# Attention on one Trainium2 core: the plain query is left unnormed, its inverse norm becomes the scale of the exponential, and the rotated query part takes the quotient of both norms

## The reference, cut to what matters

```python
def mla_qk_norm(x, gain):
    return jnp.concatenate([rms_norm(x[..., :MLA_NOPE], gain[:MLA_NOPE]),
                            rms_norm(x[..., MLA_NOPE:], gain[MLA_NOPE:])], axis=-1)
...
    q = (rms_norm(cq, q_norm) @ w_uq).reshape(b, t, MLA_HEADS, MLA_NOPE + MLA_ROPE)
    q = mla_qk_norm(q, q_gain)
...
def attend(q, k, v):
    s = jnp.einsum('bqhd,bkhd->bhqk', q, k, preferred_element_type=jnp.float32) * (q.shape[-1] ** -0.5)
    p = jax.nn.softmax(s, axis=-1).astype(v.dtype)
    return jnp.einsum('bhqk,bkhd->bqhd', p, v)
```

## Time and profile before

| | |
|---|---|
| median of 3 runs | 3030.11 us (3029.92 to 3032.5) |
| profiled execution | 3029.51 us, its span 3027.9 us |
| PE busy | 2984.7 us (99%) |
| DVE busy | 1806.4 us (60%) |
| ACT busy | 859.6 us (28%) |
| POOL busy | 37.3 us (1%) |
| chain that ended last | PE 93%, DVE 4%, ACT 1%, issue 1%, DMA 1% |

### The profile page before, as it was taken

How to read it: one execution, slowest core, us unless ns; L and a number is a source line. 1 busy time by engine, 2 the same in 40 slices (tenths; PEclk the granted TensorE clock), 3 DMA queues, 4 the chain that set the end, 5 groups by cost and what they waited for, 6 DMA issues and landing times.

```text
span 3027.9 us, 42295 instructions
## 1 busy us (share of the span) xinstructions
PE 2984.7 (99%) x17472; PEld 2604.4 (86%) x17472; DVE 1806.4 (60%) x2615; ACT 859.6 (28%) x1150; POOL 37.3 (1%) x74
## 2 busy tenths in 40 slices
PE   7999999999999999999999999999999999999999
PEld 5888888888998888888888888888889888888887
DVE  5765555766676775656574556566664646554454
ACT  5111111354445421111142111113332332332221
POOL 0000000000000000000000000000000000000000
PEclk9999999999999999999999999999999999999999
DMA  6332323111101332323211223231121211122222
GB/s 268 144 129 103 111 98 110 56 53 56 56 28 57 125 138 100 123 92 116 97 70 70 97 85 123 95 113 69 56 84 42 72 53 70 70 73 94 97 97 83
DMA packets 41064, 278.08 MB, mean 92 GB/s; under 512 B 4368, under 2 KB 5648, under 8 KB 8080
## 3 DMA queue, kind: packets, MB, share of 16 engines
q1 hardware_dynamic: 31024, 205.85, 18.7%
q0 software_dynamic: 9952, 70.98, 6.5%
HBM read 274.72 MB, written 2.10 MB: 91 GB/s over the span
## 4 chain that ended last, share of the span: by engine, by line
PE 93%; DVE 4%; ACT 1%; issue 1%; DMA 1%; SPq 0%; DVEq 0%; ACTq 0%
PE ps L330 30%; PE ps L332 29%; PE ps L331 29%; PE ps L652 1%; PE ps L356 1%; DVE act_buf L1497 1%; DVE xnl L1501 1%; DMA ada_w<-ada 1%; PE ps L344 1%; DVE wl L1413 0%; PE ps L638 0%; PE ps L639 0%; ACT wh L977 0%; ACT xnh L1008 0%; DVE ssum L1476 0%
## 5 line engine op out<-in xcount | busy, mean ns | idle before, releaser
L330 PE MATMUL ps<-xnh,wl 128*128 128x512 f32 (+1 forms) x3040 | 1057.7, 348 | 11.1 <-DVE wl L1413 5.4
L331 PE MATMUL ps<-xnl,wh 128*128 128x512 f32 (+1 forms) x3040 | 1048.4, 345 | 0.0
L332 PE MATMUL ps<-xnh,wh 128*128 128x512 f32 (+1 forms) x3040 | 1047.4, 345 | 0.0
L330 PEld LDWEIGHTS ps<-xnh,wl 128*128 128x128 f32 x3040 | 577.3, 190 | 92.2 <-issue 10.3
L332 PEld LDWEIGHTS ps<-xnh,wh 128*128 128x128 f32 x3040 | 577.1, 190 | 70.1
L331 PEld LDWEIGHTS ps<-xnl,wh 128*128 128x128 f32 x3040 | 577.5, 190 | 67.7 <-issue 1.0
L977 ACT ACTIVATE wh<-raw 128x2048 fp32r<-128x2048 f32 (+2 forms) x176 | 322.7, 1833 | 552.8 <-PE ps L332 552.8
L1413 DVE TENSOR_TENSOR wl<-raw,wh 128x2048 fp32r<-128x2048 f32 (+1 forms) x178 | 393.6, 2211 | 140.7 <-ACT wh L977 140.5
L1572 DVE SCALAR_TENSOR_TENSOR h<-ps,coef,h 128x512 f32<-128x512 f32 x624 | 371.4, 642 | 105.5 <-PE ps L332 104.0
L330 PE MATMUL ps<-hidh,wl 128*128 128x512 f32 (+1 forms) x1232 | 422.2, 343 | 3.3 <-DVE h L1512 3.3
L332 PE MATMUL ps<-hidh,wh 128*128 128x512 f32 (+1 forms) x1232 | 423.3, 344 | 0.0
(11 more groups left out here) (255 smaller groups left out, 2962.4 us busy)
## 6 DMA issues: line engine op xcount, KB each, us to landing
raw<-weights SPq DMA_DIRECT2D x183, 1024.0 KB, 4.8
adaw<-ada POOLq DMA_DIRECT2D x64, 1024.0 KB, 5.1
ada_w<-ada SPq DMA_DIRECT2D x8, 1024.0 KB, 19.1
h<-x_in SPq DMA_DIRECT2D x1, 2048.0 KB, 8.7
c_act<-c_rows POOLq DMA_DIRECT2D x2, 1024.0 KB, 5.8
out<-h SPq DMA_DIRECT2D x8, 256.0 KB, 2.0
h<-x_in SPq DMA_DIRECT2D x1, 1024.0 KB, 28.6
cs<-rope_mla POOLq DMA_DIRECT2D x1, 512.0 KB, 3.7
```

Source lines behind the costliest of these rows:

```text
L330: mm(dst, lhs[1][rows], rhs[0][rows], start=first, stop=False)
L331: mm(dst, lhs[0][rows], rhs[1][rows], start=False, stop=False)
L332: return mm(dst, lhs[0][rows], rhs[0][rows], start=False, stop=last)
```

## The change

Both plain queries of a pair are no longer normed. Let r be the inverse norm of a query row. Since exp(r · s − r · max s) is the exponential of the normed scores, r goes into the exponential as its scale, and the maximum is multiplied by r. The rotated part, which is added to the same scores, then has to be divided by r: it is multiplied by its own inverse norm and the plain part's norm.

- The items change places: 0 and 1 are now the plain queries, 2 the rotated part, 3 and 4 the keys. ACT writes the high part of a plain query with its gain straight out of PSUM (`take`), DVE the rest straight out of PSUM (`query_lo`).
- PE sums the squares of both plain queries into one bank (`head_sums`), ACT takes the root of all (`q_std`), and PE turns it by four matmuls so that the norms of 128 queries stand one per partition (`turned_std`). DVE takes their reciprocals (`q_inv`, 24 columns) and multiplies the rotated part's inverse norm by `q_std`.
- Two of the five spreads go, with two `scaled`, two `hi`, two `lo` from SBUF and two reciprocals of 192 columns.
- Each of the ten tiles gets a multiplication of the maximum (two for tiles of context queries), with a wait of DVE for itself ahead of it (`step`), and the exponential gets a scale from SBUF.
- On PE the rope's spread moves behind `value(0)`, the last spread ahead of `scores(0)`. On DVE `maximum(1)` moves ahead of `diagonal(0)`. ACT loads the table for the root at the start of a pair (not the first), by an instruction of its own.
- The wait `added(4)` for the last sums of the pair before stands ahead of `head_sums(0)`.

```diff
-        item_rows = [xn_plain[:, i, a:a + T] for i, a in ((0, 0), (0, T), (0, 2 * T), (1, 5376), (0, 5376))]
+        item_rows = [xn_plain[:, i, a:a + T] for i, a in ((0, 0), (0, 2 * T), (0, 5376))]
...
+        q_std = nrm[:, 0, 0:T // 4]
+        q_inv = nrm[:, 2, 704:728]
+        Q_AT = (0, 8, 18, 4, 12, 22)
...
+                def head_sums(hh):
+
+                    pe.wait_ge(item_sq, c.next(item_sq))
+                    ins = quarter_sums(7, L, item_sqs[hh], T, hh == 0, hh == 1, of_head[hh])
+                    if hh:
+                        ins.then_inc(item_ms, 1)
+
+                def turned_std():
+
+                    pe.wait_ge(q_std_done, c.next(q_std_done))
+                    for rows, at, cols, mat in ((slice(0, P), 0, slice(0, P), quarter),
+                                                (slice(0, 64), 8, slice(P, P + 64), quarter),
+                                                (slice(64, P), 8, slice(0, 64), next_quarter),
+                                                (slice(0, P), 16, slice(64, 64 + P), quarter)):
+                        ins = mm(ps[rows, 7, 448 + at:456 + at], q_std[:, cols], mat, start=True, stop=True)
+                    ins.then_inc(q_turned, 1)
...
-                project(0, lambda k: w(s0, k * 384 + 256), cq, 3)
+                project(0, lambda k: w(s0, k * 384), cq, 3)
...
-                project(1, lambda k: w(s0, k * 384), cq, 3)
-                item_sum(1, L, item_sqs[0], mat=ones64)
-                turned_half(item_rows[0], 0)
+                project(1, lambda k: w(s0, k * 384 + 128), cq, 3)
...
-                added()
+                    pe.wait_ge(item_v, c.next(item_v))
+                added(4)
+                head_sums(0)
+                project(2, lambda k: w(s0, k * 384 + 256), cq, 3)
+                head_sums(1)
                 pe.wait_ge(w_ready[s1], c.next(w_ready[s1]))
-                project(2, lambda k: w(s1, k * 512), ckv, 2)
-                item_sum(3, L, item_sqs[1])
+                pe.wait_ge(item_ready, c.next(item_ready, 3 if first else 1))
+                project(3, lambda k: w(s1, k * 512), ckv, 2)
+                item_sum(5, L, item_sqs[0], mat=ones64)
+                turned_half(item_rows[0], 4)
+                pe.wait_ge(item_ready, c.next(item_ready))
+                project(4, lambda k: w(s1, k * 512 + P), ckv, 2)
+                turned_std()
+                item_sum(1, L, item_sqs[1])
+                pe.wait_ge(item_rot, c.next(item_rot))
+                value(0)
                 if first:
-                    pe.wait_ge(item_v, c.next(item_v))
                     pe.wait_ge(heads_full, 16)
-                added()
                 item_spread(0, heads=True)
-                pe.wait_ge(item_rot, c.next(item_rot))
-                project(3, lambda k: w(s0, k * 384 + 128), cq, 3)
-                item_sum(5, L, item_sqs[0])
+                item_sum(3, L, item_sqs[0])
+                value(1)
                 pe.wait_ge(item_v, c.next(item_v))
                 item_spread(1)
-                project(4, lambda k: w(s1, k * 512 + P), ckv, 2)
-                item_sum(1, L, item_sqs[1])
+                pe.wait_ge(v_ready, c.next(v_ready))
+                value(2)
                 pe.wait_ge(item_v, c.next(item_v))
...
-                pe.wait_ge(item_ready, c.next(item_ready, 4 if first else 3))
+                pe.wait_ge(item_ready, c.next(item_ready, 3 if first else 2))
                 scores(0, *TILES[0])
-                pe.wait_ge(item_v, c.next(item_v))
-                item_spread(0)
                 scores(1, *TILES[1])
...
                 act.wait_ge(item_full, c.next(item_full))
-                fn(item_sqs[n_item % 2], both(n_item), ACT.Square)
+                ins = fn(item_sqs[n_item % 2], both(n_item), ACT.Square)
...
                 if between is not None:
                     root(*between)
-                if n_item:
-                    ins = fn(item_rows[n_item], both(n_item), ACT.Copy)
+                if n_item < 2:
+                    fn(qn[:, 0, n_item, :], both(n_item), ACT.Identity, scale=v("qg_nope")).then_inc(item_hi, 1)
+                elif n_item == 2:
+                    fn(item_rows[0], both(n_item), ACT.Identity, scale=v("qg_rope")).then_inc(item_sq, 1)
                 else:
-                    ins = fn(item_rows[n_item], both(n_item), ACT.Identity, scale=v("qg_rope"))
-                ins.then_inc(item_sq, 1)
+                    fn(item_rows[n_item - 2], both(n_item), ACT.Copy).then_inc(item_sq, 1)
...
+                    at = Q_AT[q + i] + hh
+                    src = ps[:, 2 * b:2 * b + 2, :].rearrange("p b t -> p (b t)")[:, 0:T] if q < 4 else ps[:, 2 * b + i, 0:L]
+                    n_key = T if q < 4 else L
+                    ins = fn(p_row(n)[:, L * i:L * i + n_key], src, ACT.Exp, bias=row[:, 0, b, i:i + 1], scale=q_inv[:, at:at + 1],
+                             accum_out=row[:, 1, b, i:i + 1])
                 ins.then_inc(exp_done, 1)
...
             def pair(first=False, last=False):
+                if not first:
+                    sqrt_table()
                 take(0)
                 take(1)
-                root(ROPE, 1)
-                take(2, (NOPE, 3, L, 1, 1))
                 if first:
                     hi(krr[:, 0, :], pre_kv[:, 3, :])
+                take(2)
+                act.wait_ge(item_ms, c.next(item_ms))
+                fn(q_std, ps[:, 7, L:L + T // 4], ACT.Sqrt, bias=eps[:, 0:1], scale=1.0 / NOPE).then_inc(q_std_done, 1)
+                take(3, (ROPE, 5))
+                take(4, (NOPE, 1, L, 1, 1))
...
+                value(0)
+                root(NOPE, 3)
                 act.wait_ge(item_v, c.next(item_v))
                 for hh in range(2):
                     own = slice(ROPE * hh, ROPE * hh + ROPE)
                     ins = fn(qrr[own, hh, :], item_rows[0][own], ACT.Copy)
                 ins.then_inc(item_hi, 1)
-                take(3, (NOPE, 5))
-                hi(qn[:, 0, 0, :], item_rows[1])
-                take(4, (NOPE, 1, L, 1, 1))
-                hi(kn[:, 0, 0, :], item_rows[2])
-
...
-                value(0)
-                root(NOPE, 3)
+                value(1)
                 split_hi(s0, 1024)
-                value(1)
-                hi(qn[:, 0, 1, :], item_rows[3])
+                hi(kn[:, 0, 0, :], item_rows[1])
                 value(2)
                 exponent(0, *TILES[0])
                 exponent(1, *TILES[1])
...
-                nc.vector.tensor_reduce(out_, in_, AX_X, ALU.max, negate=True).then_inc(max_done, 1)
+                step(nc.vector.tensor_reduce(out_, in_, AX_X, ALU.max, negate=True))
+                for i in range(1 if q < 4 else 2):
+                    at = Q_AT[q + i] + hh
+                    ins = tt(row[:, 0, b, i:i + 1], row[:, 0, b, i:i + 1], q_inv[:, at:at + 1], ALU.mult)
+                ins.then_inc(max_done, 1)
...
+                def query_lo(hh):
+
+                    dve.wait_ge(item_hi, c.next(item_hi))
+                    flat = ps[:, 2 * hh:2 * hh + 2, :].rearrange("p b t -> p (b t)")[:, 0:T]
+                    stt(out=qn[:, 1, hh, :], in0=flat, scalar=gate_cols["qg_nope"], in1=qn[:, 0, hh, :].bitcast(F32),
+                        op0=ALU.mult, op1=ALU.subtract).then_inc(item_ready, 1)
+
...
                 if first:
                     dve.wait_ge(tab_full, 16)
                     rotated(pre_kv[:, 3, :], 5)
-                inverse()
-                rotated(item_rows[0], 0)
-                if first:
                     scaled(pre_kv[:, 3, :], None)
-                scaled(item_rows[0], None)
-                inverse(1)
+                query_lo(0)
+                query_lo(1)
                 if first:
                     lo(krr[:, 1, :], krr[:, 0, :], pre_kv[:, 3, :])
+                rotated(item_rows[0], 4)
+                dve.wait_ge(item_std, c.next(item_std))
+                nc.vector.reciprocal(inv[0], inv[0])
+                dve.wait_ge(q_turned, c.next(q_turned))
+                step(nc.vector.reciprocal(q_inv, ps[:, 7, 448:472]))
+                tt(inv[0], inv[0], q_std, ALU.mult).then_inc(item_inv, 1)
+                inverse(1)
+                value(0)
+                scaled(item_rows[0], None)
+                inverse()
                 dve.wait_ge(item_hi, c.next(item_hi))
                 for hh in range(2):
                     own, other = (slice(ROPE * g, ROPE * g + ROPE) for g in (hh, 1 - hh))
                     ins = tt(qrr[other, hh, :], item_rows[0][own], qrr[own, hh, :].bitcast(F32), ALU.subtract)
                 ins.then_inc(item_ready, 1)
-                scaled(item_rows[1], gate_cols["qg_nope"])
-                inverse()
-                lo(qn[:, 1, 0, :], qn[:, 0, 0, :], item_rows[1])
-                inverse(1)
+                scaled(item_rows[1], gate_cols["kg_nope"])
+                value(1)
+                lo(kn[:, 1, 0, :], kn[:, 0, 0, :], item_rows[1])
+                value(2)
```

(8 more changed lines are left out.)

110 lines of the change are left out of this document (53 added, 57 removed).

## The result

The changed kernel takes 3038.92 us (median of 10 runs, 3036.46 to 3039.72) against 3030.66 us for the kernel before on the same chip (10 runs, 3028.74 to 3032.5). The ratio is 1.0027, 95% interval 1.0019 to 1.0035. The profiled execution took 3038.89 us, its span 3037.2 us, 9.3 us more than before. This lies outside the range of the prediction.

The account below looks back on a forecast made before the run. PE, busy 99% of the span, was taken to bound the kernel. Three pairs at −0.56 us and the first at +1.1 gave −0.6 us, a median of 3029.5 us from 3030.11; range 3021 to 3036.

Parts of the forecast that it names:

- Everything else is hidden: In the pairs: beyond the four new waits, 2.5 us per pair, other new work such as query splits and table load costs nothing.
- The rivals: Whole kernel: faster if the new waits don't form, 3021 us, chance 0.15; slower if tiles' round trip bounds, 3036.7, 0.12.
- the slower one: Rival: all ten tiles feel the added DVE and ACT work, +1.8 us per pair, 3036.7 us in all; chance 0.12.
- turning group: Four fp32 matmuls of 8 columns on PE that turn the norms: 0.85 us per pair, bounds 0.4 and 1.4.
- wait ahead of the last spread: New wait 1: PE waits 0.8 us for DVE's scaled first key, a chain of 5.7 us against 4.93 of PE work.
- ahead of the first scores: New wait 2: PE waits 0.5 us for a copy and subtraction, 1.9 us against the spread's 1.39.
- ahead of the third scores: New wait 3: PE waits 0.8 us for the first exponentials, since the last spread no longer gives them time.
- from first to fourth turn: New wait 4, in the tiles: dearer maxima on DVE cost 0.4 us at the fourth turn, bounds 0.2 and 0.8.
- pair: Each of pairs 2 to 4: −2.78 + 0.85 − 1.13 + 2.5 = −0.56 us.
- The first pair: Its head_sums(0) waits 1.05 us for bank 7; with the other terms the pair gets +1.1 us longer.
- One old wait: Old PE waits around the rope's spread were to go: 1.13 us in each later pair, 0.54 in the first.
- The clock: New waits leave it whole in the pairs; it may fall otherwise behind the attention, 3.4 us either way, chance 0.14.

Follow-up runs that it names:

- experiment 1: The kernel before with an unused tile of 32 columns (128 bytes) behind mats, moving all later tiles: 3039.18 us against 3030.23, ratio 1.003.
- experiment 2: The changed kernel with an unused tile of 32 columns behind mats, so later tiles stand 256 bytes behind their old place: 3031.52 us, ratio 1.0005.
- the seventh experiment: The kernel of experiment 2 without the multiplication of the maxima and the scale in the exponentials: 3026.6 us (one run).
- experiment 5: The kernel before with 32 unused columns between hidh and hidl, so that of the streamed tiles hidl alone moves: 3037.41 us.

## Why the prediction was wrong, by its steps

**The step that failed** is the sentence "Everything else is hidden", and with it the first one of the sum, that the change lies in the pairs alone. The wider `mats` stands among the constants of the change and was given no price. It moved the tiles that PE streams in all four feed-forward blocks, and cost 9 us: experiment 1 shows it alone, experiment 2 the change without it. There, with the tiles at their places of before, the changed kernel takes 3031.52 us against 3030.23 on that chip, +1.3 by the medians and +0.8 by the spans (+0.4 in the stretch of the attention with its inputs), where the sum said −0.6: within the bounds of −4 to +4 us that it was given. The rivals missed it as well: the slower one named 3036.7 us, near the result, but for a cause that was not at work.

**The terms of the sum**, read from the second experiment's kernel, whose places are those of before:

| term, second pair | forecast | measured |
|---|---|---|
| PE at the first turn, against before | −0.96 | 33.88 − 34.84 = −0.96 |
| turning group | 0.85 | 0.75 |
| wait ahead of the last spread | 0.8 | 1.00 |
| ahead of the first scores | 0.5 | 0.40 from start to start, under 0.2 marked |
| ahead of the third scores | 0.8 | 0.54 |
| from first to fourth turn | 0.4 | 10.36 − 9.59 = 0.77 |
| behind the fourth turn | 0 | 41.46 − 41.46 = 0 |
| pair | −0.56 | −0.19, and −0.39 in the third pair |

(Times of turns are from the pair's first projection; the fourth stands at 44.24 us against 44.43, 782.96 − 738.72 and 780.34 − 735.91.)

*The turning group.* In the changed kernel it runs from 756.02 to the sum at 756.77:

```profile
756.02 0.82 PE L713 MATMUL ps<-mats,nrm 128*128 128x8 f32 x8
756.77 0.53 PE L350 MATMUL ps<-xn_plain,mats 128*32 128x192 f32 x8
```

0.75 us, between the 0.85 that the sum took (the row had 0.81) and the 0.65 that the rule on half loads gave. The Trainium skill, page "TensorE: Matmul & The Clock Gate", section "LDWEIGHTS (loading the stationary operand)", says that a weight load takes as long as it has columns. The loads' own records (PEld) agree in their differences: 188 ns on average at 128 columns, 134 at 64 and 108 at 32, that is 54 ns for 64 columns and 26 for 32. The time of the group is more than its loads, and no plain test of that rule: the four records with 64 columns start in pairs, at 756.230, 756.237, 756.310 and 756.316.

*The chain to the last spread.* The chain was right and 0.1 us longer than summed; PE came to it 0.1 us earlier. On DVE:

```profile
760.37 0.95 DVE L1761 TENSOR_TENSOR xn_plain<-xn_plain,ps 128x768 f32<-128x768 f32 x1
...
763.09 1.92 DVE L1874 TENSOR_TENSOR qrr<-xn_plain,qrr 64x768 fp32r<-64x768 f32 x2 [0.42 <-ACT qrr L1287]
765.04 1.01 DVE L1763 SCALAR_TENSOR_TENSOR xn_plain<-xn_plain,vec,ps 128x768 f32<-128x768 f32 x1
```

and on PE:

```profile
766.18 1.68 PE L362 MATMUL ps<-irms,mats 128*128 128x192 f32 x10 [1.00 <-DVE xn_plain L1763]
767.98 0.39 PE L336 MATMUL ps<-kn,qn 128*128 128x256 f32 x1
```

From 760.37 to 766.18 are 5.81 us, for which I had 5.7. `scaled` with a gain takes 1.01, not the 0.95 of the one without. The distance 767.98 − 766.18 = 1.80 holds the 0.4 us of the second wait, of which the profile marks little, as with the old one in the earlier trace rows.

*The third scores.* The forecast had the maximum 1.5 us behind the start of the scores, the product at 2.5 and the exponentials done at 3.75:

```profile
769.47 0.69 DVE L1805 TENSOR_REDUCE row<-ps 128x2 f32<-128x512 f32 x1
770.20 0.23 DVE L1808 TENSOR_TENSOR row<-row,nrm 128x1 f32<-128x1 f32 x2
```

```profile
770.46 0.57 ACT L1244 ACTIVATE nrm<-ps,row,nrm 128x256 f32<-128x256 f32 x1 [1.74 <-DVE row L1808]
...
771.47 0.20 ACT L1244 ACTIVATION_READ_ACCUMULATOR nrm<-ps,row,nrm 128x1 f32 x1
```

Measured from 767.98: 1.49, 2.45 and 3.69 us, and the third scores start at 3.74. Every link came out. Only PE's own two tiles of scores were longer, 3.2 us instead of 2.95 (from the row below and 767.98: 771.72 − 0.54 − 767.98), so that the wait is 0.54 and not 0.8, and the start of the third scores the same. With this quarter of a microsecond the measured terms close as well: −2.78 + 0.75 − 1.13 + 1.00 + 0.40 + 0.54 + 0.25 = −0.97 at the first turn.

```profile
771.72 0.50 PE L336 MATMUL ps<-kn,qn 128*128 128x512 f32 x1 [0.54 <-ACT nrm L1244]
```

The pointer for the scale lengthens the exponential of 256 columns from 0.47 to 0.57 us, the 0.10 that the earlier trace rows gave.

*The tiles.* The 0.4 us were 0.77, of which the seventh experiment shows 0.48 to come from the small operations. Of the rest, 0.23 stand ahead of the second turn, with the small operations or without them: it starts 0.35 us behind the start of the last score product in the kernels of the second and the seventh experiment (775.48 − 775.13 and 773.09 − 772.74), 0.12 before (773.39 − 773.27). In both, DVE ends the split of the first tile just ahead of it (at 775.43 and 773.04); what makes the split late was not settled. The slower rival, that all ten tiles feel the small operations, did not happen: behind the fourth turn the pair takes as long as before.

*The first pair.* The bank that `head_sums` waits for cost 1.09 us, forecast 1.05. One old wait stayed, 0.3 us for the reciprocal ahead of the rope's spread (`irms`), which I had counted as gone. The first pair came out at +1.37 instead of +1.1.

**The clock** came out as expected: 1.00 in the pairs with waits of 1.0 us, and the same total at the lower level.

So in the pairs the waits stood where they were forecast, each within 0.4 us, and the pair's −0.19 us against −0.56 came mostly from the tiles; the time was wrong because wider constants, which look free in the code, moved other tiles.

## What to carry to other kernels

When a change alters the size of any tile, list which tiles are allocated behind it and by how many bytes they move; if PE streams one of them thousands of times, a small share of each matmul adds up: here 1 to 2% in the moved groups made 9 us, where the change itself was forecast at 0.6. Before judging such a change, run the kernel before with an unused tile of the same size, and the changed one with its tiles put back: the two runs part the place from the idea. A wait that is removed from a chain on one engine is worth only what the next wait of the same chain leaves over, so reorder the whole chain at once, and put what nobody waits for last.

## What the runs showed of the hardware

- The pace of a matmul that streams 512 columns depends on where the streamed tiles lie in SBUF modulo 256 bytes: 228.6 to 231.2 ns at one place and 232.3 to 234.1 at another (one run), on the same work. With nothing but an unused tile added, the whole kernel takes 3029.9 to 3046.4 us, 0.5%. Why, and why xnh and xnl are paced at 227 to 228 ns at theirs, stays open.
- The place of one tile changes the pace of matmuls that stream another, with which they alternate: with hidl alone moved, hidh,wl goes from 228.6 to 232.5 ns (experiment 5, one run).
- A second pointer operand, the scale, costs an exponential 0.09 to 0.10 us at 256 columns and at 768 alike: 0.99 us at 768 columns against 0.90 before.

```profile
772.41 0.99 ACT L1244 ACTIVATE sqb<-ps,row,nrm 128x768 f32<-128x768 f32 x1 [0.74 <-DVE row L1808]
```

```profile
770.19 0.90 ACT L1219 ACTIVATE sqb<-ps,row 128x768 f32<-128x768 f32 x1 [2.00 <-DVE row L1782]
```

The first row is of the changed kernel, the second of the kernel before.
